# The front step moved to the head of each attention step on TensorE

## The reference: what is computed

```python
z = h @ p["w_in"][l]
q = (rmsnorm(zq, p["g_q_norm"][l]) @ p["w_uq"][l]).reshape(B, L, MLA_HEADS, MLA_NOPE + MLA_ROPE)
kv = (lat_all @ p["w_ukv"][l]).reshape(B, -1, MLA_HEADS, MLA_NOPE + MLA_V)
# A) 8 heads: softmax(scale * (q k), masked by chunks of 64) @ v
# B) 4 heads of retention: decayed q k, a carried state, group norm and a gate
# C) 4 heads of "stick-breaking" attention
log_beta = jax.nn.log_sigmoid(zz)
log_1mb = jnp.where(mask, log_beta - zz, 0.0)
after = lax.cumsum(log_1mb, axis=3, reverse=True) - log_1mb
w = jnp.where(mask, jnp.exp(log_beta + after), 0.0).astype(sv_all.dtype)
mix = jnp.concatenate([mla_out, ret_out, sb_out], axis=-1) @ p["w_o"][l]
```

## Time and profile before

| | us |
|---|---|
| median of 3 runs | 1782.06 |
| lowest, highest | 1781.98, 1783.7 |
| the profiled execution | 1783.8 |
| its span | 1782.1 |
| blocks 0 to 7 in it | 399.6 to 788.9 |

### The profile page before, as it was taken

How to read it: one execution, slowest core, us unless ns; L and a number is a source line. 1 busy time by engine, 2 the same in 40 slices (tenths; PEclk the granted TensorE clock), 3 DMA queues, 4 the chain that set the end, 5 groups by cost and what they waited for, 6 DMA issues and landing times.

```text
span 1782.1 us, 27943 instructions
## 1 busy us (share of the span) xinstructions
PE 1671.7 (94%) x10051; PEld 1498.6 (84%) x10051; DVE 1060.8 (60%) x2269; ACT 645.0 (36%) x1252; POOL 179.6 (10%) x235
## 2 busy tenths in 40 slices
PE   6699999989788999999998999999999999999996
PEld 3499999835556677777898999999999999999996
DVE  5843333237687766767525666666666666666657
ACT  7522211225555656667424422221222122212213
POOL 0011111122333212311120000000000000000000
PEclk9899999978889999999999999999999999999999
DMA  9264444431121101005410111111111111111003
GB/s 347 81 233 153 137 129 141 136 108 37 40 92 47 43 16 47 4 13 173 148 48 13 48 48 60 36 47 35 59 35 47 35 59 35 47 35 59 12 1 113
DMA packets 114423, 133.63 MB, mean 75 GB/s; under 512 B 15003, under 2 KB 91722, under 8 KB 113002
## 3 DMA queue, kind: packets, MB, share of 16 engines
q1 hardware_dynamic: 110953, 121.83, 21.2%
q0 software_dynamic: 3328, 10.73, 1.7%
q10 hardware_dynamic: 64, 0.07, 0.0%
HBM read 107.54 MB, written 27.29 MB: 76 GB/s over the span
## 4 chain that ended last, share of the span: by engine, by line
PE 85%; DVE 7%; ACT 4%; issue 3%; DMA 1%; SPq 0%; DVEq 0%; ACTq 0%; POOLq 0%
PE psum L2002 33%; PE psum L2066 15%; PE psum L1783 13%; PE psum L1971 5%; PE psum L1924 3%; PE psum L1868 2%; PE psum L1953 2%; PE psum L1928 2%; PE psum L1822 1%; PE psum L1817 1%; PE psum L1718 1%; PE psum L1849 1%; PE psum L1719 1%; DVE h_lo L1356 1%; DVE act_lo L1356 1%
## 5 line engine op out<-in xcount | busy, mean ns | idle before, releaser
L2002 PE MATMUL psum<-act_hi,wt_parts 128*128 128x362 f32 (+1 forms) x2496 | 615.6, 328 | 9.5 <-DVE act_lo L1356 5.2
L1655 DVE SCALAR_TENSOR_TENSOR residual<-psum,mod,residual 128x364 f32<-128x364 f32 (+2 forms) x704 | 299.8, 496 | 257.6 <-PE psum L2066 257.6
L2002 PEld LDWEIGHTS psum<-act_hi,wt_parts 128*128 128x128 f32 x2496 | 442.3, 189 | 12.2 <-issue 6.8
L2002 PE MATMUL psum<-act_lo,wt_parts 128*128 128x362 f32 (+1 forms) x1248 | 409.0, 328 | 0.0
L2066 PE MATMUL psum<-u_hi,wt_parts 128*128 128x362 f32 (+1 forms) x1056 | 263.3, 331 | 3.0 <-issue 3.0
L2002 PEld LDWEIGHTS psum<-act_lo,wt_parts 128*128 128x128 f32 x1248 | 235.6, 189 | 0.0
L2066 PEld LDWEIGHTS psum<-u_hi,wt_parts 128*128 128x128 f32 x1056 | 188.1, 189 | 3.3 <-issue 3.3
L1783 PE MATMUL psum<-w_hi,h_hi 128*128 128x308 f32 (+1 forms) x576 | 177.6, 308 | 12.1 <-DVE h_lo L1356 10.9
L1783 PE MATMUL psum<-w_lo,h_hi 128*128 128x308 f32 (+1 forms) x576 | 177.0, 307 | 0.0
L1783 PE MATMUL psum<-w_hi,h_lo 128*128 128x308 f32 (+1 forms) x576 | 176.5, 306 | 0.0
L2066 PE MATMUL psum<-u_lo,wt_parts 128*128 128x364 f32 (+1 forms) x528 | 174.7, 331 | 0.0
(11 more groups left out here) (222 smaller groups left out, 2289.3 us busy)
## 6 DMA issues: line engine op xcount, KB each, us to landing
wt_raw<-in_w_up SPq DMA_DIRECT2D x44, 512.0 KB, 3.8
ada_raw<-in_w_ada SPq DMA_DIRECT2D x32, 512.0 KB, 4.1
wt_raw<-in_w_down SPq DMA_DIRECT2D x22, 512.0 KB, 4.3
w_raw<-in_w_in SPq DMA_DIRECT2D x16, 616.0 KB, 6.9
z_scratch<-z_out POOLq DMA_DIRECT2D x64, 154.0 KB, 2.3
z_in<-z_scratch SPq DMA_DIRECT2D x8, 1232.0 KB, 5.3
ada_first<-in_w_ada SPq DMA_DIRECT2D x16, 512.0 KB, 11.5
xT_scratch<-xT SPq DMA_DIRECT2D x1, 4352.0 KB, 15.6
```

What stands on the lines that cost most here:

```text
L1655: last = dve.scalar_tensor_tensor(out=res[:, d, a:b], in0=bank[4 + q % 4][:, a - CHUNKS[c][0]:b - CHUNKS[c][0]], scalar=mod[:, 40 + d, whi ...
L2002: last = pe.matmul(out[:, :b - a], ww[:, slot, P * k:P * k + P], aa[:, k, a:b], start=(k == 0 and m == 0), stop=(k == KT - 1 and m == 2))
```

## The change

In the loop of TensorE, the cache step (only ahead of block 0) and the front step go from the end of each step to its beginning.

```diff
             for step in range(-12, STEPS):
                 m, s = divmod(step + 12, 12)
+                if m == 0:
+                    cache_step(s)
+                if m < NTILE:
+                    front(m, s)
                 if 0 <= step < len(UNITS):
                     scores(step)
                 for x in PIECES.get(step - 1, []):
@@
                 for x in PIECES.get(step, []):
                     transposes(x)
-                if m == 0:
-                    cache_step(s)
-                if m < NTILE:
-                    front(m, s)
```

## The result

The changed kernel takes 2074.8 us (median of 4 runs, 2067.3 to 2086.6) against 1782.7 us before: 1.164 times as long, 95% interval 1.158 to 1.171. The forecast was 2037 us. The profiled execution took 2079.2 us, its span is 2077.5.

A forecast was written before the change was run, and what follows sets the result against it. TensorE, 85% of the chain of waits, was taken to bound the kernel, so added waits are paid in full. 1782 us plus 189 of waiting plus 66 of clock loss gave 2037 us, range 1935 to 2150.

The forecast's parts named there:

- cover theory: Blocks 0 to 7: nothing stands between one step's transposes and the next front to cover bank 7's readers; +189 us waiting.
- The hand-overs: Bank 7, blocks 0 to 7: 30.3 us of waits per wide block, 27 per narrow, 228 in place of 38.9.
- The clock: TensorE in blocks 0 to 7: longer waits bring more time at 1.2 GHz, +66 us, mean clock about 0.75.
- lower clock throughout: Rival: attention's TensorE work runs at half clock throughout, +235 us in place of +66, 2206 us; chance 0.13.
- Half price: Rival: ScalarE-ended chains mostly hidden, no clock lost, mainly the five VectorE-ended steps paid; +114, about 1896 us; chance 0.10.
- no change: Rival: readers of bank 7 are done before TensorE's transposes, so the time stays the same; chance 0.01.
- The faster case: Rival: at the block's edge an earlier front lets VectorE start its chain earlier; -50, 1732 us; chance 0.02.
- The Trainium skill's rule: TensorE's front and pieces: transposes not counting as clock activity would favour the colder case, 2206 us.

The follow-up runs named there:

- the filled run: Changed kernel plus extra multiplications of 256 columns, results never read, behind TensorE's transposes to fill its waits: 1961.0 us, ratio 1.099 to the kernel before.

## Why the prediction was right, and where it was not

**The mechanism held.** All orders but TensorE's are unchanged, the growth lies where the front steps are, and the chain is the one named: transposes, copies of the pieces, front copy, VectorE's part, next front. The runs with cover put back, and with the reads moved ahead, each moved the time as the cover theory has it.

**The hand-overs, step by step.** In block 6 the measured waits ahead of the next front, with the forecast in brackets: step 0 5.3 (6.7), 1 1.0 (1.4), 2 5.0 (3.8), 3 2.0 (2.3), 4 2.2 (2.5), 5 1.4 (1.5), 6 0 (0.6), 7 1.2 (1.5), 8 1.2 (1.5), 9 2.2 (2.5), 10 0.6 (0.8), 11 5.0 (5.2). Sum 27.2 of 30.3 (that of step 5 holds 0.26 ahead of the transposes of the joined outputs). Most come out 0.1 to 0.4 low: the profile counts a wait from the modelled end of the transposes, and where ScalarE is last TensorE starts 0.05 us behind it (946.10, against 945.45 + 0.60), where I had allowed 0.15. Two steps are off for a reason that I had not seen, GpSimd's work beside VectorE's (below): it makes step 2 longer than forecast, and its absence makes step 0 shorter.

Over the eight blocks I forecast 228 us of waits and the trace has 194.9. I had taken block 6 for all wide blocks, but the waits are 20.2 us in block 0, 24.8 to 27.2 in blocks 4 to 7 and 23.0 to 23.6 in the narrow ones, where I had 27. Some of what VectorE needs also lies beside work of TensorE that had become slower; the filled run, at 0.98, has at most 230.9.

**The clock was mis-sized.** The forecast gave it 66 us, with 100 as its own upper bound; TensorE's same work took 137.0 us more, and holding the clock up gave at least 114 us back. The step that failed is the one in which I let only waits of about 3 us count and gave wide blocks two more dips of 3.4 us each. In fact the clock lay between 0.60 and 0.73 in every block, wide or narrow (block 6: 0.69), and the stretch of block 6 without a wait above 2.3 us had 0.69 too. The row that told so was in my hands: 0.55 from 384.0 to 405.0 with waits of about a microsecond. I used it for a rival instead of for the forecast. The rival "lower clock throughout" was too cold: 0.50 would have been the whole stretch at 1.2 GHz, 0.68 was measured, and I had expected about 0.75; the time, 2075, lies nearer to 2037 than to 2206.

**That the time came out so near is partly luck.** The added waits were 33 us under the forecast (156 of 189) and the clock's share 71 us over it (137 of 66), so half of the second error was covered by the first.

**The other rivals.** Half price and no change need ScalarE's and VectorE's reads to be early, and the ScalarE rows above show that they cannot be. The faster case needs VectorE to take up a front at the edge as soon as it is ready. In its unchanged order it can't: in block 6 front step 11 is finished at 963.31, and VectorE, idle until 964.74, first does its maximum and its sums and begins the retention chain at 968.99. With its reads moved as well the kernel was still 0.9% slower than before.

**The Trainium skill's rule** that transposes do not count as activity (TensorE: Matmul & The Clock Gate, Part 4: PE-mode transpose) did not decide: the same transposes stood in the stretch of block 6 that ran at 1.00 before, beside scores and weighing. With the gaps filled by ordinary multiplications the changed kernel's stretch ran at 0.98, and no run here filled them with transposes, so whether they count stays open.

## What to carry to other kernels

Where one buffer is handed round between engines, look not at how early its producer stands but at what stands on the producer's queue between the last thing its readers must wait for and its next use: that cover was 3.25 us per step in block 6 here, and taking it away cost 292 us without one instruction more. Ask whether the other engines of the chain can move with it: moved on TensorE alone the front step cost 16%, on all three engines 0.9%. And price the clock by a stretch of the trace with the same pattern of work and waits, not by the longest wait: in the stretch of block 6 above, 8.4 us more of waits of one to two microseconds came with 15.3 us more of the same work, and over all blocks it was 137 us beside 156.

## What the runs showed that I had not expected

**GpSimd holds VectorE up.** In step 2 of block 6 of the changed kernel, VectorE's last rotation operation takes 1.55 us, not the usual 0.29:

```profile
895.84 1.55 DVE L1465 TENSOR_TENSOR qtok<-q_a,q_b 128x128 f32<-128x128 f32 x1
```

and GpSimd's subtraction for the stick-breaking weights runs at that time:

```profile
895.44 1.80 POOL L816 TENSOR_TENSOR esb<-zsb,esb 128x768 f32<-128x768 f32 x1 [9.88 <-DVE esb L1537]
```

It starts when VectorE's sums end, and VectorE's operation is done 0.15 us behind it. Of the 16 such operations in the blocks (mean 388 ns before, now 666, together 4.5 us more) seven are long, all in step 2 and so on the path. Each of the seven begins beside a GpSimd subtraction and ends 0.14 to 0.15 us behind it, whether that lasts 0.72 us (VectorE's then takes 0.47) or 2.07 us (1.82); the nine without one take 0.29.

The edge shows the opposite. Before, VectorE's end of the retention in step 0 ran beside a GpSimd operation and took 1.23 us:

```profile
732.20 1.27 POOL L783 TENSOR_TENSOR rqk<-rope_a,rope_b 128x512 f32<-128x512 f32 x1
```

In the changed kernel GpSimd is done by then, and the same operation takes 0.43:

```profile
874.98 0.43 DVE L1499 TENSOR_TENSOR oc<-oc,stat 128x256 f32<-128x256 f32 x1 [3.88 <-ACT stat L1061]
```

VectorE's part there, from L1499 to the end of L1453, shrank from the 3.2 us that I had put into the sum to 2.1, most of the 1.4 us by which step 0 came out short. No run took GpSimd's work away, so that it is the cause is read from these coincidences and not tested by an experiment.

**More work, less time.** 386 multiplications whose results nobody reads made the changed kernel 114 us faster. As a cure it is a poor one (moving the reads gave 274 us), but as a measurement it puts a bound on what the clock costs and one on what the waits cost.
